# Expert pairs of a two-layer MoE step: down of one pair behind gate and up of the next

## What is computed

```python
def _hier_moe(h, w_group, w_expert, w_gate, w_up, w_down):
    p_group = jax.nn.softmax((t @ w_group).astype(F32), axis=-1)
    g_sel = jnp.argmax(p_group, axis=-1)
    ...
    top_v, top_i = lax.top_k(e_in, TOP_K)
    w_top = jax.nn.softmax(top_v, axis=-1) * p_g
    expert_id = g_sel[:, None] * EXP_PER_GROUP + top_i
    ...
    hid = jax.nn.silu(jnp.einsum('td,edf->tef', t, w_gate)) * jnp.einsum('td,edf->tef', t, w_up)
    out = jnp.einsum('tef,efd->td', hid * combine.astype(h.dtype)[:, :, None], w_down)
```

## Time and profile before

| | |
|---|---|
| median of 3 runs | 1308.36 us (1308.15 to 1311.05) |
| the profiled execution, its time | 1308.29 us |
| its span, first to last instruction | 1306.4 us |
| mean granted clock of TensorE | 0.981 of full speed |
| TensorE busy | 1190.0 us, 91% of the span |
| VectorE, ScalarE, GpSimd busy | 590.4, 350.1, 186.5 us |
| mean DMA rate over the span | 202 GB/s, 263.50 MB |
| expert stage of the first layer | about 627 to 771 us |
| expert stage of the second layer | about 1101 to 1260 us |

### The profile page before, as it was taken

The page is one execution under the profiler, slowest core; times in us unless marked ns, Lnnn a source line. Parts: engine busy times, 40 slices in busy tenths (PEclk is TensorE's granted clock), DMA queues, the critical chain, the costliest instruction groups (busy, mean ns, idle before and its releaser), DMA issues.

```text
span 1306.4 us, 17530 instructions
## 1 busy us (share of the span) xinstructions
PE 1190.0 (91%) x6771; PEld 690.7 (53%) x6771; DVE 590.4 (45%) x1171; ACT 350.1 (27%) x693; POOL 186.5 (14%) x177
## 2 busy tenths in 40 slices
PE   4999999999999989999998788999999998997784
PEld 2554455545446677455564445655554555664441
DVE  2222332310236666857232116089986855322118
ACT  1334444411315444211221115220033121221122
POOL 1000000010000001130333110800000311351210
PEclk9999999999999999998999999999999999999988
DMA  9513558865010207406999958121115028999953
GB/s 349 201 63 137 191 199 295 281 212 186 15 65 9 69 9 273 176 33 263 364 408 405 395 189 343 44 83 43 63 65 209 33 105 337 408 411 403 363 218 154
DMA packets 97938, 263.50 MB, mean 202 GB/s; under 512 B 12619, under 2 KB 14962, under 8 KB 96962
## 3 DMA queue, kind: packets, MB, share of 16 engines
q1 hardware_dynamic: 81904, 228.26, 46.3%
q0 software_dynamic: 15632, 34.02, 7.1%
q10 hardware_dynamic: 322, 0.12, 0.0%
HBM read 254.53 MB, written 28.79 MB: 217 GB/s over the span
## 4 chain that ended last, share of the span: by engine, by line
PE 72%; SPq 10%; DMA 7%; DVE 6%; ACT 3%; issue 3%; ACTq 0%; DVEq 0%; POOLq 0%
PE ps L2216 17%; PE ps L2227 14%; PE ps L2728 5%; DMA scratch<-in_moe_w_up 4%; SPq L697 3%; SPq L699 3%; PE ps L2106 3%; PE ps L2368 3%; PE ps L2531 2%; PE ps L2745 2%; SPq L696 2%; PE ps L2677 2%; DMA mix_cm<-in_mod_w 2%; PE ps L2512 2%; PE ps L2335 2%
## 5 line engine op out<-in xcount | busy, mean ns | idle before, releaser
L2216 PE MATMUL ps<-h_cm,weights 128*128 128x512 f32 (+1 forms) x832 | 226.8, 434 | 0.0
L2216 PEld LDWEIGHTS ps<-h_cm,weights 128*128 128x128 f32 x832 | 126.3, 191 | 104.0 <-issue 103.7
L2227 PE MATMUL ps<-weights,mix_cm 128*128 128x512 f32 x256 | 112.2, 595 | 0.0
L1719 DVE SCALAR_TENSOR_TENSOR scratch<-scratch,taps_cm 128x655 f32<-128x655 f32 x120 | 101.5, 897 | 2.5 <-ACT scratch L1289 1.0
L2227 PEld LDWEIGHTS ps<-weights,mix_cm 128*128 128x128 f32 x256 | 47.9, 190 | 56.5 <-issue 56.4
L2011 DVE TENSOR_TENSOR scratch<-ps,scratch 128x128 f32<-128x128 f32 x38 | 11.1, 291 | 145.8 <-ACT scratch L1329 145.8
L2728 PE MATMUL ps<-weights,scratch 128*64 128x256 f32 x544 | 64.0, 388 | 12.7 <-DMA weights<-in_moe_w_up 8.7
L2227 PE MATMUL ps<-weights,h_cm 128*128 128x512 f32 (+1 forms) x208 | 71.4, 502 | 0.0
L2728 PE MATMUL ps<-h_cm,scratch 128*64 128x256 f32 x240 | 56.2, 389 | 11.0 <-DMA scratch<-in_moe_w_up 8.2
L2728 PEld LDWEIGHTS ps<-weights,scratch 128*64 128x64 f32 x544 | 43.9, 140 | 34.9 <-issue 12.3
L1392 DVE COPY mod_parts<-ps 128x512 f32<-128x512 f32 x24 | 16.6, 690 | 93.5 <-PE ps L2106 93.5
(11 more groups left out here) (437 smaller groups left out, 2044.4 us busy)
## 6 DMA issues: line engine op xcount, KB each, us to landing
weights<-in_mod_w SPq DMA_DIRECT2D x13, 2048.0 KB, 8.9
x_tm<-in_mod_w SPq DMA_DIRECT2D x10, 2048.0 KB, 8.6
weights<-in_moe_w_gate SPq DMA_DIRECT2D x34, 512.0 KB, 8.4
weights<-in_moe_w_up SPq DMA_DIRECT2D x34, 512.0 KB, 10.6
weights<-in_moe_w_down SPq DMA_DIRECT2D x34, 512.0 KB, 11.1
weights<-in_ab_w_in SPq DMA_DIRECT2D x5, 2048.0 KB, 12.8
weights<-in_cd_w_in SPq DMA_DIRECT2D x5, 2048.0 KB, 15.9
scratch<-in_moe_w_down SPq DMA_DIRECT2D x18, 512.0 KB, 11.5
```

Of the source, the lines that this page charges most:

```text
L1719: ins = V.scalar_tensor_tensor(out=CO[:, j, 0:655], in0=UP[:, j, k:k + 655], scalar=CW[:, 4 * k + j:4 * k + j + 1], in1=CO[:, j, 0:655], o ...
L2216: ins = T.matmul(ps(*name)[:, a:b], w[:, k, col:col + 128], HT[:, k, a:b], start=(k == 0), stop=(k == KD - 1))
L2227: ins = T.matmul(ps(*name)[:, at:at + w.shape[2]], src[:, k, t * 128:t * 128 + 128], w[:, k, :], start=(k == 0), stop=(k == KD - 1))
```

## The change

In the sixteen main pairs `down` of a pair moves one stage back. TensorE now goes through gate_up(u), turn of u+1, down(u-1), turn_hidden(u), and does the last `down` behind the loop. The result copies on ScalarE (`first_half`) and VectorE (`second_half`) and GpSimd's scatter follow in the same way, one pair behind. SyncE asks for the weights in that order too: gate and up of u, then `down` of u-1 (`load_downs`). The extra pairs keep their old order of work (`behind` is 0 there), but their waits on `x_slot` become (1, 3, 3, 4) in place of (1, 2, 3, 4), since ScalarE now counts gate and up of pair 12 ahead of `down` of pair 11. TensorE gets two waits ahead of the gate broadcast. VectorE's block `weights_of_pairs` stays in round 4, and comes ahead of the result copy of pair 4.

```diff
@@ -751,6 +751,12 @@
...
             load_expert(l, 2 * u + i, u % RING, i, pair_gu[u % RING], pair_down[u % RING], parts)
+        def load_downs(u):
+            at_least(sp, m["down"], u - RING + 1)
+            for i in range(2):
+                if (u, i) not in ((1, 1), (2, 0), (2, 1)):
+                    load_main(u, i, (1,))
+
         load_main(1, 1)
         load_main(2, 0)
...
@@ -766,11 +772,13 @@
...
                 sp.wait_ge(d_hst[0], 16 * 3 * (l + 1))
                 sp.wait_ge(d_hst[1], 16 * 2 * (l + 1))
-            for part, read in enumerate((m["gu"], m["down"])):
-                at_least(sp, read, u - RING + 1)
-                for i in range(2):
-                    if (u, i) not in ((1, 1), (2, 0), (2, 1)):
-                        load_main(u, i, (part,))
+            at_least(sp, m["gu"], u - RING + 1)
+            for i in range(2):
+                if (u, i) not in ((1, 1), (2, 0), (2, 1)):
+                    load_main(u, i, (0,))
+            if u:
+                load_downs(u - 1)
+        load_downs(NP0 - 1)
         quads = sp.value_load(RI[0:1, 0:1], min_val=0, max_val=NEXTRA // 4)
...
@@ -779,7 +787,7 @@
...
                     for part in range(2):
-                        sp.wait_ge(m["x_slot"], j * 4 + (2 * p + part + 1))
+                        sp.wait_ge(m["x_slot"], j * 4 + (1, 3, 3, 4)[2 * p + part])
                         for i in range(2):
                             load_expert(l, pair[i], 1 + p, i, m[f"xw{p}"], m[f"xwd{p}"], (part,))
...
@@ -912,19 +920,22 @@
...
         pool.wait_ge(rows_ready, 2 * l + 2)
         pool.wait_ge(d_mod, MOD_DMAS * 2)
+        def scatter_main(u):
+            pool.wait_ge(m["ya"], u + 1)
+            pool.wait_ge(m["yv"], u + 1)
+            at_least(pool, m[f"s{u % 2}"], 16 * (u // 2))
+            scatter(u % 2, TIY[:, 1, u:u + 1])
+
         for u in range(NP0):
-            par = u % 2
             if u in (6, 8):
                 residual_rows(u // 2)
...
             if u < NP0 - 2:
                 gather(u % 4, TIY[:, 0, u + 4:u + 5])
-
-            pool.wait_ge(m["ya"], u + 1)
-            pool.wait_ge(m["yv"], u + 1)
-            at_least(pool, m[f"s{par}"], 16 * (u // 2))
-            scatter(par, TIY[:, 1, u:u + 1])
+            if u:
+                scatter_main(u - 1)
+        scatter_main(NP0 - 1)
         pool.dma_start(GATE_ROW, MODD[l, 3:4].rearrange("i g c -> i (g c)")).then_inc(d_r5, 16)
         if l:
...
@@ -1318,7 +1329,15 @@
...
             A_(XGT[:, u % 2, 0:512], turned_bank(0), ACT.Copy).then_inc(m["xa"], 1)
-        def pairs(n0, s0, count, frees):
+        def first_half(n0, s0, u, frees):
+
+            act.wait_ge(m["down"], n0 + (u + 1))
+            if u in frees:
+                act.sem_inc(m["x_slot"], 1)
+            at_least(act, m[f"s{u % 2}"], s0 + 16 * (u // 2))
+            A_(ZT[:, u % 2, 0:512], result_bank(u, 0), ACT.Copy).then_inc(m["ya"], 1)
+
+        def pairs(n0, s0, count, frees, behind):
             turned(n0, 0)
             for u in range(count):
...
@@ -1329,20 +1348,18 @@
...
                 if u + 1 < count:
                     turned(n0, u + 1)
-
-                act.wait_ge(m["down"], n0 + (u + 1))
-                if u in frees:
-                    act.sem_inc(m["x_slot"], 1)
-                at_least(act, m[f"s{u % 2}"], s0 + 16 * (u // 2))
-                A_(ZT[:, u % 2, 0:512], result_bank(u, 0), ACT.Copy).then_inc(m["ya"], 1)
+                if u >= behind:
+                    first_half(n0, s0, u - behind, frees)
+            if behind:
+                first_half(n0, s0, count - 1, frees)
         emptied(act, "tb", l)
-        pairs(0, 0, NP0, (NP0 - 5, NP0 - 4))
+        pairs(0, 0, NP0, (NP0 - 5, NP0 - 4), 1)
         act.wait_ge(rt_ready, l + 1)
         quads = act.value_load(RI[0:1, 0:1], min_val=0, max_val=NEXTRA // 4)
         with act.If(quads > 0):
             with act.Fori(0, quads) as j:
-                pairs(j * 2 + NP0, j * 16 + 8 * NP0, 2, (0, 1))
+                pairs(j * 2 + NP0, j * 16 + 8 * NP0, 2, (0, 1), 0)
         def broadcast(kind, dst):
...
@@ -2002,33 +2019,44 @@
...
             V.tensor_copy(XGT[:, u % 2, 512:1024], turned_bank(1)).then_inc(m["xv"], 1)
-        def pairs(n0, s0, count):
+        def second_half(n0, s0, u):
+
+            dve.wait_ge(m["down"], n0 + (u + 1))
+            at_least(dve, m[f"s{u % 2}"], s0 + 16 * (u // 2))
+            V.tensor_copy(ZT[:, u % 2, 512:1024], result_bank(u, 1)).then_inc(m["yv"], 1)
+
+        def pairs(n0, s0, count, behind):
             turned(n0, 0)
             for u in range(count):
...
                 at_least(dve, m["ht"], n0 + (u - 1))
                 V.tensor_tensor(HID[:, u % 2, :], pair_bank(u)[:, 128:256], SG[:, u % 2, :], ALU.mult).then_inc(m["hid"], 1)
+                if behind:
+                    if u + 1 < count:
+                        turned(n0, u + 1)
+                    if u:
+                        second_half(n0, s0, u - 1)
                 dve.wait_ge(m["ht"], n0 + (u + 1))
                 at_least(dve, m["down"], n0 + (u - 1))
                 V.tensor_copy(HIDT[:, u % 2, :], pair_bank(u)[:, 256:384]).then_inc(m["hc"], 1)
-                if u + 1 < count:
-                    turned(n0, u + 1)
-
-                dve.wait_ge(m["down"], n0 + (u + 1))
-                at_least(dve, m[f"s{u % 2}"], s0 + 16 * (u // 2))
-                V.tensor_copy(ZT[:, u % 2, 512:1024], result_bank(u, 1)).then_inc(m["yv"], 1)
-                if count == NP0 and u == 4:
+                if not behind:
+                    if u + 1 < count:
+                        turned(n0, u + 1)
+                    second_half(n0, s0, u)
+                if behind and u == 4:
                     weights_of_pairs()
+            if behind:
+                second_half(n0, s0, count - 1)
         extra_blocks()
-        pairs(0, 0, NP0)
+        pairs(0, 0, NP0, 1)
         dve.wait_ge(rt_ready, l + 1)
         quads = dve.value_load(RI[0:1, 0:1], min_val=0, max_val=NEXTRA // 4)
         with dve.If(quads > 0):
             with dve.Fori(0, quads) as j:
-                pairs(j * 2 + NP0, j * 16 + 8 * NP0, 2)
+                pairs(j * 2 + NP0, j * 16 + 8 * NP0, 2, 0)
         if l == 0:
...
@@ -2753,6 +2781,11 @@
...
             return u % RING
+        def main_down(u):
+            p = u % RING
+            pe.wait_ge(pair_down[p], 32 * (uses(p, l) + u // RING + 1))
+            down(0, u, slot_of_main)
+
         main_turn(0)
         for u in range(NP0):
...
@@ -2760,9 +2793,10 @@
...
             if u + 1 < NP0:
                 main_turn(u + 1)
+            if u:
+                main_down(u - 1)
             turn_hidden(0, u)
-            pe.wait_ge(pair_down[p], 32 * (uses(p, l) + u // RING + 1))
-            down(0, u, slot_of_main)
+        main_down(NP0 - 1)
         pe.wait_ge(rt_ready, l + 1)
...
@@ -2787,6 +2821,8 @@
...
         pe.wait_ge(d_r5, 16 * (l + 1))
+        pe.wait_ge(m["ya"], quads * 2 + (NP0 - 1))
+        pe.wait_ge(m["yv"], quads * 2 + (NP0 - 1))
         for h in range(2):
             broadcast_row("gate", l, h, const("ones")[0:1, 0:128], GATE_ROW)
...
```

## The result

The kernel before took 1309.99 us (median of 6 runs, 1308.15 to 1311.05), the changed one 1316.70 (6 runs, 1315.23 to 1316.97). The ratio is 1.0049, with a 95% interval from 1.0037 to 1.0061: the change makes the kernel slower by 6.7 us. The profiled execution of after took 1316.74 us, with a span of 1314.8. That of before took 1308.29, which is 1.7 us under the median of its kernel; that of after stands at its median.

What follows compares the result with a forecast made beforehand. Bytes queued ahead of each layer's last gate-and-up load were taken to bound the expert stages, not TensorE. The sum 1308.29 + 2.60 + 2.58, all other terms 0, gave 1313.47, predicted as 1313.5; range 1305.0 to 1317.5.

Steps and rivals of the forecast that it cites:

- rival 4: Last gate and up of each layer starts at TensorE's lower clock level, costing 1.69 us each: 1316.9; chance 0.05.
- TensorE's period: TensorE's time per main pair falls from 7.02 to about 6.6 us; worth to the whole time costed at nothing.
- The megabyte: Pair 3's `down` requests leave the hole (near-idle DMA before each full stretch) for the full queue: 2.60 and 2.58 us.
- The later frees: SyncE's queue: `down` slots freed one stage later hold gate and up behind them, yet it never runs dry: 0.
- the extra pairs: Second layer's second quad: first `down` loads asked 4.4 us later, costed at 0 with an upper end of 4.
- the other engines: VectorE, ScalarE and GpSimd do the same work, with result copies and scatter one stage later: all 0.
- The first (the megabyte absorbed): Tails of the expert stages absorb the moved megabyte in both layers, 1308.3, or in one, 1310.9; chance 0.28.
- The second (TensorE's period decides): TensorE's shorter period, not the loads, decides to the end of both stages: 1294.5; chance 0.08.
- The third (the second quad starves): Second layer's second quad: its `down` loads come after the engines drained, up to 4 us more: 1317.5; chance 0.07.

Runs made afterwards that it cites:

- e2: The changed kernel with SyncE's weight requests put back in the old order, the other engines keeping the new order of work; ratio to before 0.9997.
- e1: The changed kernel run once more with no edit; ratio to before 1.0055.
- e4: The changed kernel with the `down` requests of pairs 3 and 4 back right behind their own gate and up; ratio to before 1.0019.
- e5: The kernel before, with only 16 columns of pair 3's `down` matrices loaded in each layer; ratio to before 0.9987.
- e6: The changed kernel, with only 16 columns of pair 3's `down` matrices loaded in each layer; ratio to before 1.0007.
- e10: The changed kernel with ScalarE's gate-and-up count moved behind the result copy, so the `x_slot` waits are (1, 2, 3, 4) again; ratio to before 1.0047.
- e12: e2 with pair 4's `down` also asked ahead of the router wait and one more unneeded matmul in the first layer; ratio to before 1.0010.
- e9: e4 with one unneeded matmul before pairs 13, 14 and 15, and two (second layer one) before the second extra pair; ratio to before 1.0004.
- e3: The kernel before with only SyncE's requests in the changed kernel's order, all work in the old order; ratio to before 1.0031.
- e8: The kernel before with pair 4's `down` also asked behind pair 3's loads, ahead of the router wait; ratio to before 0.9977.
- e11: e8 with one more unneeded matmul in the first layer, while TensorE waits for the router; ratio to before 0.9979.

## Why the prediction was right, and what it missed

**The number.** The sum was 1313.5, and the median is 1316.70, inside the stated range but above the band of 1311.5 to 1315.5 that the forecast kept for itself. Two things make up the 3.2 us. The sum started from 1308.29, the profiled execution, and the median of before over six runs is 1309.99: 1.7. The median rose by 6.7 and not by 5.2: 1.5. What was right is the mechanism and its 5.2; that the range also took in the rest was its width. 1316.7 is also next to the 1316.9 of rival 4, by chance: its two groups, the last gate and up of each layer, take 3.68 and 3.67 us in after, at the upper level.

**TensorE's period.** Right in its worth, off in its size. It went to 6.82 us and not to 6.6: the 0.43 of waiting went, but gate and up take 3.60 in place of 3.45 and the turn of the hidden rows 0.26 in place of 0.11. The gain was costed at nothing, and e2 shows nothing. TensorE's lead only lengthened its waits: 1.69 us before pair 10 (none) and 4.75 before pair 11 (3.79), where the forecast had 8.4 before pair 11 alone, 1.95 before pair 15 (1.01), 2.75 before the last pair (1.35, forecast 2.4).

**The megabyte.** The step that carried the forecast, 2.60 + 2.58 = 5.2. e1 has 2.6 + 2.5, e4 takes back all of it by two requests, and e5 and e6 show both halves of the argument: free in the hole, 2.6 us behind it. The burst ahead of the hole is shorter, as said: the engines are busy for 0.72 of those seven microseconds and not all of them, about 2 us less. Pair 11 came near 709 and pair 15 near 746; the last gate and up at 768.05 is later than the 766.8 forecast by 1.3, which is how much later this execution's first gate and up started (628.97, 627.63 before). In e1, whose first one starts at 627.55, it stands at 766.80. In the second layer the last one is at 1262.31 and at 1260.04 in e1, where 1258.5 was forecast. Of the 3.8 us that after is later, 1.3 are its later start, 1.7 stand between the stages, and 0.9 in the second layer, where pair 16's gate and up took 5.36 us in after and 3.67 in e1.

The figure of the Trainium skill (DMA: Bandwidth & Descriptors, Where 436 GB/s comes from), about 358 GB/s between HBM and SBUF for a core, would have made a megabyte cost an estimated 2.93 us. After's stretches at 403 and 402 GB/s speak against it again; the same section also names a transfer of 16 MB that was measured at 425 GB/s, which these rates are nearer to. The 2.5 and 2.7 us of e6's first layer, against after and e1, agree with 2.60.

**The later frees, the extra pairs, the other engines.** Costed at 0 and measured at 0, for this kernel: e4 (a full queue doesn't mind the order in it), e10 and e2. e12 shows what the first of these zeros hangs on, the megabytes that stand in line in front.

**Rivals.** The first (the megabyte absorbed) falls with e6: the mean share of 0.49 from 755 to 764 was no room. More bytes do pass there in after (265 GB/s for 189), and the last gate and up is 2.5 us later all the same. The second (TensorE's period decides) falls with pair 11 at 709.41. The third (the second quad starves) is half seen: the share of its stretch is 0.87 (317 GB/s) where it was 1.00 (374), but without its wait (e10: 0.95, 363 GB/s) the time is the same. The fourth (the last gate and up at the lower level) didn't occur in after, e1 or e10.

**The clock, the missing term.** The median rose by 6.7 and the sum had 5.2. In the profiled executions the rest stands between the stages, 1.7 us in after and 1.6 in e1. The forecast looked for the clock only at the last gate and up of each layer, as a rival with a chance of 0.05, and priced the whole stretch between the stages at nothing, for no work changes there. But what follows a stage starts at another moment and after other waits, and after and e1 lose at different places. Three stretches of before, after and e1, laid at the same distance from the last gate and up (36 and 30 us long):

```profile
764.00:800.00 36.00, 30.64 (x99) 13.90 (x99) 16.10 (x27) 10.17 (x18) 3.47 (x5) 0.95 0.69 259
800.00:830.00 30.00, 29.02 (x210) 24.77 (x211) 8.12 (x26) 15.54 (x38) 11.79 (x7) 1.00 0.42 160
```

```profile
768.00:804.00 36.00, 30.81 (x100) 14.05 (x101) 16.20 (x27) 10.25 (x18) 2.47 (x5) 0.95 0.69 261
804.00:834.00 30.00, 29.04 (x206) 25.54 (x207) 8.02 (x25) 15.61 (x37) 10.31 (x6) 0.95 0.42 157
```

```profile
767.00:803.00 36.00, 32.03 (x99) 14.28 (x95) 14.98 (x27) 9.04 (x15) 2.26 (x3) 0.91 0.70 262
803.00:833.00 30.00, 27.88 (x207) 24.26 (x208) 9.25 (x26) 16.68 (x41) 10.66 (x7) 1.00 0.41 155
```

After loses in the second stretch (granted 0.95 for 1.00), e1 in the first (0.91 for 0.95). In after it is visible at 803.89, in the fence of TensorE's time line: 8 transposes take 1.94 us after an idle 2.54. The same ones of before:

```profile
800.03 1.07 PE L2167 MATMUL ps<-consts,x_tm 128*128 128x128 f32 x8 [2.53 <-ACT h_cm L1029]
```

In e1 it is the gate broadcast, whose 8 matmuls take 5.12 us at 773.88 and 3.69 in before and in after. Behind these places after is 1.7 us and e1 1.6 us behind before, so a lower level there accounts for all that the stretch lost. e9 shows that filling waits can remove such a loss, but no run removed this one from after itself. So the 1.6 is read from the granted clock, not shown by an edit of its own.

Nor is it shown that the change causes it. e5, whose work and requests stand in the order of before and whose stages are as long, has 338.6 between them, with the same transposes slow:

```profile
801.91 1.94 PE L2169 MATMUL ps<-consts,x_tm 128*128 128x128 f32 x8 [2.53 <-ACT h_cm L1031]
```

e3, with the requests of after, has 337.4. And the one execution of before that was profiled is 1.7 us under its kernel's median, so other executions of before may lose here as well. All three profiled executions with the change in full (after, e1, e10) have 338.8 to 338.9; whether the stretch is 1.6 us longer in the median too stays open.

## What to carry to other kernels

Ask of every request that an edit moves in an in-order queue whether it crosses a place where the queue is stuck and the engines run dry: here the bytes that crossed it cost their full transfer time at the end of the stage, and bytes that changed places within a full queue cost nothing. Look at which requests stand ahead of a long wait before giving any worth to an engine that gets faster while it waits for loads; and once that is found, try the other direction, since here one pair's `down` more in the hole (e8) was worth 2.6 us. Take the waits that remain as a risk to TensorE's clock of some 1.5 us for each place (1.4 to 1.7 here), and measure the stretches behind a changed stage as well as the stage. Two executions don't start a stage at the same moment, so move the windows of a table by that much before comparing them: at fixed times the burst and the hole of after read 342 and 32 GB/s, and 293 and 96 at equal distance from the first gate and up.

## What was not expected of the hardware

**The same idle time does not give the same clock.** Idle 2.53 and 2.54 us before the same eight transposes gave 1.07 and 1.94 us; idle 2.72 and 2.75 before the same last gate and up gave 5.38 (e4) and 3.69 (after). In e9, with 0.63 idle there, it was 3.70. The last gate and up repeats by kernel: 3.67 in e1 and e10 too, after 2.74 and 2.76, and 5.37 in e6 after 2.75. So the length of a wait before a group doesn't tell its speed alone, and what else does is open. The Trainium skill (TensorE: Matmul & The Clock Gate, HAM oscillation) describes a kernel whose matmuls wait for loads in every round and are throttled again after each wait; its waits were longer than these four, so they don't test it. The longer ones here agree with it: after 3.79 us in before and 4.75 in after, pair 11's gate and up took 5.36 and 6.47.

**A mended place may give its gain back.** e11's one matmul more won 1.6 us in the first layer, and its profiled execution lost 1.5 at the gate broadcast, 140 us later, with nothing changed in between. The ratios of e8 and e11 are the same (0.9977 and 0.9979). That the one caused the other isn't shown: e5 lost as much in that stretch with nothing mended.

**A full hole isn't quite free.** With the second megabyte in it, the gathered rows that the first pair needs came later: from the first gather to the first turn it is 5.48 us in e8 and 4.70 in before, and TensorE waits 1.11 us for them.
